# Ten norm halves of a two-layer trunk: one fp32 product with ones, root and reciprocal on all partitions, in place of three column sums and three spreading products

## What is computed

```
def _rmsnorm(x, gain):
    xf = x.astype(jnp.float32)
    y = xf * lax.rsqrt(jnp.mean(xf * xf, axis=-1, keepdims=True) + EPS)
    return (y * gain.astype(jnp.float32)).astype(x.dtype)
...
        def modulated(j, y):
            return _rmsnorm(y, g[j]) * (1 + mod[:, :, 3 * j + 1]) + mod[:, :, 3 * j]

        x = x + 0.5 * mod[:, :, 2] * _swiglu(modulated(0, x), ffn_w_in[l, 0], ffn_w_out[l, 0])
        h = modulated(1, x)
...
        x = x + mod[:, :, 5] * out
        x = x + 0.5 * mod[:, :, 8] * _swiglu(modulated(2, x), ffn_w_in[l, 1], ffn_w_out[l, 1])
```

## Time and profile before

| | us |
|---|---|
| median of 3 runs | 2317.88 |
| lowest, highest | 2317.43, 2319.32 |
| the profiled execution | 2317.71 |
| its span in the trace | 2315.6 |
| TensorE busy in it | 2298.5 (99%) |
| VectorE busy | 1600.5 (69%) |
| ScalarE busy | 979.2 (42%) |

### The profile page before, as it was taken

The page is one execution under the profiler, slowest core; times in us unless marked ns, Lnnn a source line. Parts: engine busy times, 40 slices in busy tenths (PEclk is TensorE's granted clock), DMA queues, the critical chain, the costliest instruction groups (busy, mean ns, idle before and its releaser), DMA issues.

```text
span 2315.6 us, 39357 instructions
## 1 busy us (share of the span) xinstructions
PE 2298.5 (99%) x16336; PEld 2220.4 (96%) x16336; DVE 1600.5 (69%) x2391; ACT 979.2 (42%) x1567; POOL 30.6 (1%) x44
## 2 busy tenths in 40 slices
PE   8999999999999999999999999999999999999999
PEld 8999999988889999999999999999998999999999
DVE  6886776658867876776587767676765668467473
ACT  5433423443656523414364144144545455244242
POOL 0000000000001000000010000000000010000000
PEclk9999999999999999999999999999999999999999
DMA  9352554421101252444215444324133012322122
GB/s 303 128 164 83 190 164 144 148 90 55 58 20 55 92 164 95 143 128 146 92 55 183 128 146 133 105 83 161 55 107 98 19 55 79 104 73 94 58 95 74
DMA packets 200267, 252.89 MB, mean 109 GB/s; under 512 B 13122, under 2 KB 174746, under 8 KB 199962
## 3 DMA queue, kind: packets, MB, share of 16 engines
q1 hardware_dynamic: 199666, 250.20, 32.9%
q10 hardware_dynamic: 424, 0.18, 0.0%
HBM read 245.76 MB, written 3.28 MB: 108 GB/s over the span
## 4 chain that ended last, share of the span: by engine, by line
PE 92%; DVE 3%; ACT 2%; DMA 2%; issue 1%; SPq 1%; POOL 0%; DVEq 0%; ACTq 0%
PE banks L1184 80%; PE banks L1337 1%; PE banks L1514 1%; PE banks L1516 1%; PE banks L1515 1%; DMA w_raw<-ffn_w_in 1%; PE banks L1661 1%; PE banks L1673 1%; PE banks L1688 1%; DMA mod_first<-w_mod 1%; ACT w_hi L2163 1%; DVE w_lo L2885 0%; SPq L1145 0%; SPq L942 0%; DVE w_raw L2906 0%
## 5 line engine op out<-in xcount | busy, mean ns | idle before, releaser
L1184 PE MATMUL banks<-b_hi,w_hi 128*128 128x320 f32 x2496 | 776.8, 311 | 3.7 <-DVE work L3251 2.2
L1184 PE MATMUL banks<-b_hi,w_lo 128*128 128x320 f32 x2496 | 772.4, 309 | 0.0
L1184 PE MATMUL banks<-b_lo,w_hi 128*128 128x320 f32 x2496 | 772.2, 309 | 0.0
L2163 ACT ACTIVATE w_hi<-w_raw 128x1024 fp32r<-128x1024 f32 x317 | 332.5, 1056 | 424.1 <-PE banks L1184 236.2
L2885 DVE TENSOR_TENSOR w_lo<-w_raw,w_hi 128x1024 fp32r<-128x1024 f32 x317 | 387.3, 1224 | 163.4 <-ACT w_hi L2163 161.8
L1184 PEld LDWEIGHTS banks<-b_hi,w_hi 128*128 128x128 f32 x2496 | 468.7, 188 | 16.4 <-issue 10.6
L1184 PEld LDWEIGHTS banks<-b_lo,w_hi 128*128 128x128 f32 x2496 | 468.8, 188 | 0.0
L1184 PEld LDWEIGHTS banks<-b_hi,w_lo 128*128 128x128 f32 x2496 | 468.7, 188 | 0.0
L1184 PE MATMUL banks<-hid_hi,w_hi 128*128 128x320 f32 x1664 | 400.4, 312 | 0.5 <-DVE hid_lo L3189 0.5
L1184 PE MATMUL banks<-hid_hi,w_lo 128*128 128x320 f32 x1664 | 396.6, 309 | 0.0
L1184 PE MATMUL banks<-hid_lo,w_hi 128*128 128x320 f32 x1664 | 396.5, 309 | 0.0
(11 more groups left out here) (383 smaller groups left out, 2422.8 us busy)
## 6 DMA issues: line engine op xcount, KB each, us to landing
w_raw<-ffn_w_in SPq DMA_DIRECT2D x176, 512.0 KB, 4.8
mod_grain<-w_mod SPq DMA_DIRECT2D x78, 512.0 KB, 5.8
w_raw<-ffn_w_out SPq DMA_DIRECT2D x64, 512.0 KB, 4.4
last_grain<-w_mod SPq DMA_DIRECT2D x40, 512.0 KB, 5.1
w_raw<-ffn_w_out SPq DMA_DIRECT2D x32, 384.0 KB, 3.7
w_raw<-w_in_odd SPq DMA_DIRECT2D x20, 512.0 KB, 4.6
mod_first<-w_mod SPq DMA_DIRECT2D x6, 1024.0 KB, 11.8
w_raw<-w_in_even SPq DMA_DIRECT2D x12, 512.0 KB, 6.0
```

The source lines that it names most:

```text
L1184: ins = pe.matmul(o, w3[w], v3[v][cols], start=first and i == 0, stop=last and i == 2, skip_group_check=onto_read)
L2163: act.activation(ring_in(w_hi, in_slot(f, d, t)), operand(d, t), ACT.Copy).then_inc(hi_ready, 1)
```

## The change

All ten halves of norms 1 to 5 are done in another form. `wide_sums` replaces `half_sums`: one fp32 product of a 128x128 tile of ones with the half of `ss`, 320 moving columns, which leaves each token's sum of squares on all partitions in PSUM. `wide_root` takes the root of 128x320 from PSUM and writes it to `ss`. VectorE inverts in place: hf 0 in one instruction (`invert_first`, 128x320), hf 1 in two of 128x160 (`invert_second`). The spreading products, the copy to `ss` and the tile `rms` go away, and both halves are scaled from `ss`. The opening norm stays as it is.

The places change too. On TensorE the first half's product moves ahead of the last step of part(tile 6, hf 1) in `out_tail`, or ahead of its last three steps in `tail_pair`; the second half's stands ahead of block 3 in `first_double` (before: 2) and, as before, ahead of block 2 in the mixers. On VectorE the update of x's tile 6, hf 1 moves behind the reciprocal and the first scale; scale(6, 8) moves ahead of the second half's reciprocal; the second piece of that reciprocal stands behind low form 5. On ScalarE the first high form moves ahead of the square of tile 6, hf 1, and high form 2 ahead of that of tile 7.

```diff
-            def half_sums(n, hf):
+            def wide_sums(n, hf):
 
                 pe.wait_ge(square_added, half_squares(n, hf))
-                for i, (first, _, _) in enumerate(SUM_TILES):
-                    t0 = hf * HALF + first
-                    ins = pe.matmul(token_sums[hf][:, i:i + 1], ss[:, t0:t0 + P], ones[:, 0:1], start=True, stop=True)
-                ins.then_inc(sums_ready, 1)
-
-            def spread_inverse(n, hf):
-
-                pe.wait_ge(inverse_ready, 1 + norms_before(n, hf) + 1)
-                for i, (first, r0, r1) in enumerate(SUM_TILES):
-                    ins = pe.matmul(inverse_of[hf][:, first + r0:first + r1], rms[r0:r1, hf, i:i + 1].to_broadcast([r1 - r0, P]),
-                                    ident[r0:r1, r0:r1], start=True, stop=True)
-                ins.then_inc(inverse_spread, 1)
+                pe.matmul(spread_of[hf], ones[:, :], ss[:, half_of(hf)], start=True, stop=True).then_inc(sums_ready, 1)
...
-                out_part(f, c, KT - 2, 1).then_inc(w_used, 1)
-                half_sums(n, 0)
-                out_part(f, c, KT - 1, 1, lambda: spread_inverse(n, 0)).then_inc(w_used, 1)
+                out_part(f, c, KT - 2, 1, {CHUNKS[c] - 1: lambda: wide_sums(n, 0)}).then_inc(w_used, 1)
+                out_part(f, c, KT - 1, 1).then_inc(w_used, 1)
...
-                part(0, 1).then_inc(out_ready, 1)
-                half_sums(n, 0)
-                part(1, 1, lambda: spread_inverse(n, 0)).then_inc(w_used, 1)
+                part(0, 1, {HK + 1: lambda: wide_sums(n, 0)}).then_inc(out_ready, 1)
+                part(1, 1).then_inc(w_used, 1)
...
-                act.activation(rms[:, hf, :], token_sums[hf], ACT.Sqrt, scale=1.0 / D, bias=eps[:, 0:1])\
+                act.activation(ss[:, half_of(hf)], spread_of[hf], ACT.Sqrt, scale=1.0 / D, bias=eps[:, 0:1])\
                     .then_inc(rms_ready, 1)
...
-                root(n, 0)
+                wide_root(n, 0)
+                after_first(0)
                 square_half(n, KT - 2, 1, x_before)
-                for kt in range(2):
+                for kt in (1, 2):
                     after_first(kt)
                 square_half(n, KT - 1, 1, x_before)
...
-            def invert(n, hf):
-
-                dve.wait_ge(rms_ready, 1 + norms_before(n, hf) + 1)
-                dve.reciprocal(rms[:, hf, :], rms[:, hf, :]).then_inc(inverse_ready, 1)
+            def invert_first(n):
+
+                dve.wait_ge(rms_ready, 1 + norms_before(n, 0) + 1)
+                dve.reciprocal(ss[:, half_of(0)], ss[:, half_of(0)]).then_inc(inverse_ready, 1)
+
+            def invert_second(n, part):
+
+                if part == 0:
+                    dve.wait_ge(rms_ready, 1 + norms_before(n, 1) + 1)
+                cols = slice(HALF + part * HALF // INVERSE_PARTS, HALF + (part + 1) * HALF // INVERSE_PARTS)
+                dve.reciprocal(ss[:, cols], ss[:, cols]).then_inc(inverse_ready, 1)
```

In `tail_norm`, which both kinds of norm run on VectorE:

```diff
                 middle()
+                invert_first(n)
+                scale(slice(0, 1), 0)
                 last_half(KT - 2)
-                invert(n, 0)
-                scale(slice(0, 1), 0)
-                add_sq_half(n, KT - 2, 1)
                 scale(slice(1, 2), 0)
                 low(slice(0, 1), 0)
+                add_sq_half(n, KT - 2, 1)
                 scale(slice(2, 4), 0)
+                low(slice(1, 2), 0)
                 last_half(KT - 1)
-                low(slice(1, 2), 0)
+                low(slice(2, 3), 0)
                 add_sq_half(n, KT - 1, 1)
                 scale(slice(4, 6), 0)
-                low(slice(2, 3), 0)
                 low(slice(3, 4), 0)
...
-                invert(n, 1)
-                scale_form(n, f, slice(6, 8), 0)
+                scale(slice(6, 8), 0)
+                invert_second(n, 0)
                 item_lo(f, 0, 2)
                 low(slice(4, 5), 0)
                 item_lo(f, 0, 3)
                 low(slice(5, 6), 0)
+                invert_second(n, 1)
                 scale(slice(0, 2), 1)
                 low(slice(6, 8), 0)
```

More of the change, by code:

```diff
@@ L152, in trunk @@
         SUM_BANK = (6, 7)
-        token_sums = [bank[b][:, HALF:HALF + len(SUM_TILES)] for b in SUM_BANK]
-        inverse_of = [bank[b][:, 0:HALF] for b in SUM_BANK]
+        spread_of = [bank[b][:, 0:HALF] for b in SUM_BANK]
         consts_in = sem("consts_in")
@@ L1256, in first_double @@
             def first_double(f, n):
-                plain_parts(f, 0, range(2), range(2))
-                half_sums(n, 1)
-                plain_parts(f, 0, range(2, HK), range(2))
-                spread_inverse(n, 1)
-                plain_parts(f, 0, range(HK, KT), range(2))
+                plain_parts(f, 0, range(3), range(2))
+                wide_sums(n, 1)
+                plain_parts(f, 0, range(3, KT), range(2))
                 plain_parts(f, 1, range(KT), range(2))
@@ L1490, in tail_pair, with part @@
                 pe.wait_ge(lo_ready, unit + 1)
-                def part(i, hf, midway=None):
+                def part(i, hf, steps={}):
                     for k in range(KT):
-                        if midway is not None and k == 2:
-                            midway()
+                        if k in steps:
+                            steps[k]()
                         ins = split_product([(bank[TAIL_BANKS[i][hf]][:, 0:HALF], (slice(None), k, half_of(hf)))],
@@ L2102, in spread_first @@
                     if t0 < t1:
-                        ins = pe.matmul(inverse_of[hf][:, t0 - hf * HALF:t1 - hf * HALF], x_rms[:, t:t + 1].to_broadcast([P, P]),
+                        ins = pe.matmul(spread_of[hf][:, t0 - hf * HALF:t1 - hf * HALF], x_rms[:, t:t + 1].to_broadcast([P, P]),
                                         ident[:, t0 - t * P:t1 - t * P], start=True, stop=True)
@@ L2188, in sqrt_table, with wide_root, keep_first_inverse @@
                 act.activation(table_call[:, :], eps[:, :], ACT.Sqrt)
-            def root(n, hf):
+            def wide_root(n, hf):
                 act.wait_ge(sums_ready, TT + norms_before(n, hf) + 1)
-                act.activation(rms[:, hf, :], token_sums[hf], ACT.Sqrt, scale=1.0 / D, bias=eps[:, 0:1])\
+                act.activation(ss[:, half_of(hf)], spread_of[hf], ACT.Sqrt, scale=1.0 / D, bias=eps[:, 0:1])\
                     .then_inc(rms_ready, 1)
-            def keep_inverse_of(n, hf):
-                act.wait_ge(inverse_spread, 2 * n + hf + 1)
-                act.activation(ss[:, half_of(hf)], inverse_of[hf], ACT.Copy).then_inc(inverse_kept_in[hf], 1)
+            def keep_first_inverse(hf):
+                act.wait_ge(inverse_spread, hf + 1)
+                act.activation(ss[:, half_of(hf)], spread_of[hf], ACT.Copy).then_inc(inverse_kept_in[hf], 1)
             def shift_tile(n, view, kt, hf):
@@ L2246, in mix_norm @@
                 tail_squares(n, x_before, lambda: None, lambda kt: high(kt, 0))
-                shifted(2, 0)
-                shifted(3, 0)
-                rounded(2, 0)
-                rounded(3, 0)
-                root(n, 1)
+                high(3, 0)
+                wide_root(n, 1)
                 split_hi(unit, "mix")
@@ L2319, in norm_by_half @@
                 tail_squares(n, x_before, between, lambda kt: form_high(n, f, kt, 0))
-                for kt in range(2, HK):
-                    form_high(n, f, kt, 0)
-                root(n, 1)
+                form_high(n, f, HK - 1, 0)
+                wide_root(n, 1)
                 item_hi(f, 0, 2)
```

36 lines of the change are left out of this document (15 added, 21 removed).

## The result

The changed kernel takes 2330.9 us, the median of six runs (2328.7 to 2332.3), beside 2318.0 for the kernel before on the same chip (2317.0 to 2319.3). The ratio is 1.0057, with a 95% interval of 1.0047 to 1.0067: **slower by 0.57%, 12.9 us**. The forecast was +8.7 us, 2326.4, with a range of 2320.0 to 2332.5. So the direction and the range held, and 4.2 us of the loss were not forecast. The profiled execution took 2332.26 us with a span of 2330.5, 14.9 more than the 2315.6 of before.

A forecast was written before the change was run, and what follows sets the result against it. TensorE, busy for 2298.5 of 2315.6 us, was taken as the bound. About 17.8 us of new waits against 9.1 us less work, summed over five norms, gave +8.7 us, 2326.4 us, with a range of 2320 to 2332.5.

The forecast's parts named there:

- The bound: Whole kernel: TensorE busy for 2298.5 of 2315.6 us, so only work leaving its queue wins time and any wait loses it.
- The product: Each norm half on TensorE: the new fp32 product costs 0.54 + 0.14 + 0.10 = 0.78 us against the old 1.67.
- the saving: TensorE work removed by the new product: 0.9 us a half, 9 us in ten halves, bounds 5 to 10 us.
- The reciprocal: VectorE in each norm: 2.14 us for 320 columns, 1.14 for 160, from a straight line through narrower rows.
- rival A: VectorE's reciprocal costs a third more a column when wide, 2.8 us instead of 2.14: +14, 2332 us; chance 0.09.
- The root: ScalarE in each norm: 128x320 read from PSUM takes 0.44 us, priced by copy L2199, instead of 0.26 for 128x3.
- The waits: TensorE at the five norms: about 17.8 us of new waits; at 717, 0.3, 1.7, 0.5 and 0.4.
- Rival C: No waits at block 4 since ScalarE does not hold the weight tile behind the root: -9.1, 2308.6 us; chance 0.07.
- Rival B: Reciprocal runs like any other operation (0.49 us); first-form waits go, block 4 waits stay: about +0.1, 2318; chance 0.07.
- Rival D: The new product on TensorE costs 1.2 us instead of 0.78 and delays the chain: +13, 2331 us; chance 0.05.
- Behind the norms nothing gives it back: After each norm, forms and products shift together, so the +8.7 us summed at the norms stays in the total.
- weight tiles further on: VectorE falls back 0.3 us more than TensorE at three norms, which later weight tiles could feel; left to the range.

## Why the prediction was right, and where it was off

**The bound** was read rightly: at a share of 99% TensorE has no slack, and what it waits more for appears in the time.

**The product** was the mis-sized term. The prediction took 0.54 for its two records, which is what was measured, and added 0.14 for entering fp32 and 0.10 for leaving it. Neither exists beside a wide product. So the saving was 1.13 a half, 11.3 us in all, not 9. It brought next to nothing, because TensorE only came to its waits earlier: at 717 it stood ready 0.24 us sooner for a form that ended at 723.97, 5.75 us behind the start of the product where the forecast had 5.73. The first wait grew from 0.3 to 0.58. Where a chain sets the next start, an error in the price of what TensorE does meanwhile cancels.

**The reciprocal** was right, and rival A is dead: from 160 to 320 columns (1.148 to 2.152) it takes 6.3 ns a column. The 8.3 that the prediction estimated from the repeat count of 8 in the Trainium skill, page "VectorE: DVE Perf Modes", section "Walkthrough: the 8-slice pipeline in each mode", does not agree with this. **The root** was 0.09 short. It was priced by a copy from PSUM of the same shape, which is not an operation of the same kind.

**The waits** came where they were named, in the order in which they were named: at 717 four of four within 0.3 us, at 1164 2.5, 1.8, 0.5 and 0.5 where 4.8 in sum was forecast. New waits at the norms come to 19.4 us against the forecast's 17.8, and the saving to 11.3 against 9.1. Net that is 8.1 against 8.7 over the five norms; at 1609 it is 0.5 less than forecast, at 478 0.2 less.

**Rival C** (no waits at block 4) decided at one point, and the profile answers it: VectorE idles for 1.57 us until the second root is there, and the low part of tile 2 comes behind that. **Rival B** asked what is left without the reciprocal, and was run: +2.8, not +0.1. **Rival D** fell with 0.54.

**What failed** is one sentence: "Behind the norms nothing gives it back". Nothing was given back, but more was taken. The prediction named weight tiles further on as something that "could feel" the change and left them to the range. They took about 3 us more of idle time, 4 with what each wait costs beyond its bracket. What lies behind them is loads that land late, four of them with an instruction packet inside, and kernels without the reciprocals have them too. And the prediction priced a wait by its length, where a long one can be followed by some 3 us at half the clock. That cost 1.4 us in two of three profiles, about 1 us on average. Norms, weight tiles and clock are 8.1 + 4 + 1 = 13.1 us, beside 12.9 between the medians. The range took both in only because it had been drawn wide for errors at the norms that were not made, so that the total fell inside it is in part luck.

## What to carry to other kernels

Removing work from a saturated engine pays only as far as the results it waits for come earlier too: here 11.3 us of matmul work were removed, and the long reciprocals, with a second product that came one block later at three norms, made it wait 19 us longer. Before an operation is widened over all partitions, read its price per column on the engine that takes it over (the reciprocal's 6.3 ns make 2.15 us over 320 columns, where an ordinary operation takes 0.49), and look for a single operation that does both steps. Put the product that opens a chain as early in the order as its inputs allow; moving the second one by one block at three norms was worth 5.8 us between medians in the kernels with the single operation, and 2.9, within the noise, in those with the reciprocals.

## What the runs showed of the hardware that was not expected

- The granted clock can fall to 0.50 behind a wait of TensorE far shorter than the stretch at the lower level that follows, which lasted some 3 us each time. It fell in three of four cases when no matmul had started for 2.4 us, in 6 of 37 for 1.8 to 1.9 us, in 2 of 12 at the wait of 0.97. Each fall costs 1.3 to 1.7 us, and the number of falls differs between the profiles of one kernel (one, one and none in the changed one). That this makes its times scatter more is not shown: its six runs spread over 3.6 us and six of before over 2.3, but nineteen others of before over 3.9.
- Switching TensorE from the split products to fp32 and back shows no cost beside a product of 320 columns: 0.54 us for two records. Six records of one column took 0.67 in the old form, 0.11 each; whether that is the switch or a least time of a record is not shown.
- A wait of TensorE costs 0.24 to 0.27 us beyond the idle time that the profile names: 0.16 is the part of a matmul's 0.31 that the next one overlaps at the usual step of 0.147, and the rest is a longer distance to the second matmul behind the wait (0.22 to 0.25).
- Abs_reciprocal_sqrt on ScalarE over 128x320 from PSUM takes 0.53 us, as long as Sqrt.
- Four loads of 512 KB, each followed in twelve profiles: with a 16 KB packet of the instruction queue that starts 0 to 3.8 us behind the issue (33 cases) they took 5.3 to 7.2 us, without (15 cases) 4.8 to 5.3. That the packet is the cause fits all 48 and was not tested by a run of its own.
